# An MoE kernel on one core: the experts' results added in memory by the scatter, one scatter in flight

## The chip, the cores and the metric

The kernel runs on one core of a Trainium2 chip. The metric is device time in microseconds from the first to the last instruction of the launch, the median over runs. Times in the profile are those of one profiled execution.

## The reference, cut to what matters

One layer of a streaming encoder for 512 tokens of 1024 channels, in float32. First comes token mixing (projection, convolution branch, RWKV branch, merge), which the change leaves alone. Then a mixture of experts: every token picks 8 of 64 experts, each a SwiGLU of width 256, and a shared expert runs over all tokens.

```python
scores = jax.nn.sigmoid(t @ w_router)                  # choice: grouped top-8, gate = sel / sum * 2.5
expert(x) = (silu(x @ we_gate[e]) * (x @ we_up[e])) @ we_down[e]
routed = segment_sum(expert rows * gate, tok, 512)      # 512 x 8 = 4096 assignments
shared = (silu(t @ ws_gate) * (t @ ws_up)) @ ws_down
x = x + gt2 * rmsnorm(routed + shared, norm_ffn_post)
```

## The kernel before

The MoE part has four pieces, each a block of its own with a barrier at its end: `plan_experts` (buffers), `route`, `experts` and `combine`.

`route` computes scores, the choice of experts, the shared expert (kept in SBUF as `moe.shared`), and a table with three values for every token and expert: the gate, the token's number, and the number of the row 8 x token + rank in which this result is to be stored. Each value is split into three bfloat16 parts (`moe.parts`, L1795 to L1799), so that a product with a one-hot matrix picks it exactly. SP loads the weights of the first four experts at the end of this piece.

`experts` walks over blocks of up to 128 tokens of one expert: 64 first blocks, one for each expert, and a few more for experts with over 128 tokens (`n_blocks`, 68 with these inputs). A helper, `steps`, writes the same loop for every engine: a list of stages, each with a lead, so that in step b the stage of lead 4 works on block b+4. The order in the list is the order on the engine. For one block:

- DVE `places` and PE `numbers` (lead 4) pick the block's gates, token numbers and row numbers; DVE turns the last two into integers (`tokens`, `row_ids`). Places without a token get a number out of bounds, and the transfer skips them.
- POOL `gather` (lead 4, L2013): an indirect DMA reads the tokens' rows of 4 KB from memory into `xg`, one of four buffers.
- PE `turn_x`, ACT `x_high`, DVE `x_low` (lead 2): transpose, and split into a high and a low float32r part. ACT `high` and DVE `low` (lead 2) split the weights the same way; `low` writes over the loaded weights' place.
- PE `gate_up` (lead 1): 48 products of 512 columns a block; ACT and DVE make the hidden values; PE `down` (lead 0): 8 more. ACT and DVE copy the result to `y`, one of two buffers, and may do so when the scatter of two blocks before has landed (`left`).
- POOL `scatter` (lead 0, L2022): an indirect DMA writes the rows of `y` to their places in `moe.rows`, a tensor of 4096 rows in memory, so that no two writes meet. It waits for `y` and the row numbers, not for another scatter; two can be in flight. Ahead of every indirect DMA a tiny POOL operation on `carrier` carries its wait.

On POOL the order in a step is gather b+4, scatter b. In the blocks from 60 on, which may or may not exist, POOL also waits at the end of each step for the scatter's landing (`last`).

SP loads weights in a ring of four: it waits until PE is done with the gate and up of block n-4 and issues 2 MB for block n (L1863), then until PE is done with the down of block n-4 and issues 1 MB for block n (L1866), then the same for n+1. PE's gate and up run a block ahead of its down, so a down load and the next block's gate and up loads come right after each other. After the last block SP loads x1, the residual, 2 MB, into the place of ring slot 0 (L1995), which the profile names `x_again`, and waits for it.

`combine` (L2189): ten loads bring all 16 MB of `moe.rows` back, for each group of 128 tokens four rows a token for PE and four for DVE. PE adds its four and the shared expert by products with the identity, DVE adds its four in a tree, then the two. ACT squares, POOL takes the power for the norm, DVE scales by the gate row (`gated`) and adds to x1 (`finish`), and SP stores halves of 256 KB.

Of the kernel before, what the change touches and what calls it, by code (L numbers as in the profile page):

```python
# [28 lines left out]
P = 128  # L29
# [1506 lines left out]
NO_TOKEN, NO_ROW = 8 * S, 16 * S * TOPK  # L1536
# [3 lines left out]
def route(nc, w, keep, moe):  # L1540
# [4 lines left out]
    with ExitStack() as stack:  # L1545
# [29 lines left out]
        toki, tokf, pi, pf = m.sb("toki", [P, NT], I32), m.sb("tokf", [P, 3, NT]), m.sb("pi", [P, 1], I32), m.sb("pf", [P, 1])  # L1575
        iota_i = m.sb("iota_i", [P, S], I32)
        values = m.sb("table_values", [P, NT * NE, 3])
# [18 lines left out]
        def _(sp):  # L1596
# [7 lines left out]
            for b in range(moe.RING):  # L1604
                moe.load_gate_up(sp, b, b)
                moe.load_down(sp, b, b)

        @block.gpsimd
        def _(pool):
            pool.iota(toki[:, :], [[P, NT]], base=0, channel_multiplier=1).then_inc(s_io, 1)  # L1610
            pool.iota(pi[:, :], [[0, 1]], base=0, channel_multiplier=1).then_inc(s_io, 1)
            pool.iota(iota_i[:, :], [[1, S]], base=0, channel_multiplier=0).then_inc(s_io, 1)
            pool.memset(resets[:, :, :], 1.0).then_inc(s_io, 1)
            pool.memset(moe.offsets[:, 0:1], float(NO_TOKEN)).then_inc(s_io, 1)
            pool.memset(moe.offsets[:, 1:2], float(NO_ROW)).then_inc(s_io, 1)
            pool.wait_ge(s_io, 6)
            pool.memset(resets[:, :, 0:1], 0.0).then_inc(s_io, 1)

        @block.scalar
        def _(act):  # L1620
# [15 lines left out]
            for t in range(NT):  # L1636
# [8 lines left out]
                for half in range(2):  # L1645
                    act.activation(moe.shared[:, t, half * N:half * N + N], bank[6 + half][:, :], ACT.Copy).then_inc(s_dnA, 1)
# [74 lines left out]
        def _(dve):  # L1721
# [11 lines left out]
            dve.wait_ge(s_io, 7)  # L1733
# [6 lines left out]
            link.sign(V.tensor_scalar(tokf[:, 2, :], tokf[:, 0, :], float(TOPK), float(-NO_ROW), ALU.mult, ALU.add))  # L1740
# [43 lines left out]
            for t in range(NT):  # L1784
# [49 lines left out]
def plan_experts(nc, m, w, keep, moe):  # L1834

    moe.RING = 4
    with ExitStack() as first_use:
        raw = Memory(nc, first_use)
        gate_up = [moe.x1] + [raw.sb(f"gate_up{i}", [P, NT, D]) for i in range(1, moe.RING)]
    low = [moe.low0] + [m.sb(f"gate_up_low{i}", [P, 2, KD, DE], F32R) for i in range(1, moe.RING)]  # L1840
    moe.gate_up = [t[:, :, :].rearrange("p a d -> p (a d)").rearrange("p (j k n) -> p j k n", j=2, k=KD) for t in gate_up]
    moe.low = low
    moe.down = m.sb("down_ring", [P, moe.RING, 2, D])
    moe.place = m.sb("place", [P, NT, NE])
    moe.parts = m.sb("table_parts", [P, NT, NE, 3, 3], BF16)
# [4 lines left out]
    moe.offsets = m.sb("offsets", [P, 2])  # L1850
# [20 lines left out]
def experts(nc, w, keep, moe):  # L1871
# [4 lines left out]
    with ExitStack() as stack:  # L1876
# [3 lines left out]
        column = m.sb("column", [P, 2, NT, 9], BF16)  # L1880
        number = m.sb("number", [P, 4, 3])
        tokens = m.sb("tokens", [P, 4, 1], U32)
        row_ids = m.sb("row_ids", [P, 4, 1], U32)
# [17 lines left out]
        s_num, s_rows = m.sem("p5_token_numbers"), m.sem("p5_row_numbers")  # L1901
# [7 lines left out]
        s_x1 = m.sem("p5_x1_in")  # L1909
# [67 lines left out]
        def _(sp):  # L1977
            with sp.Fori(1, NE // RING) as turn:
                for u in range(RING):
# [3 lines left out]
                    moe.load_down(sp, RING * turn + u, u)  # L1983
            count = sp.value_load(moe.n_blocks[0:1, 0:1], min_val=NE, max_val=MAXB)
# [9 lines left out]
            sp.wait_ge(s_y, count)  # L1994
            sp.dma_start(moe.x1[:, :, :], keep.x1_dram.rearrange("(t p) d -> p t d", p=P)).then_inc(s_x1, 16)  # L1995
            sp.wait_ge(s_x1, 16)

        @block.gpsimd
        def _(pool):
            last_token, last_row = pool.to_reg(S - 1), pool.to_reg(S * TOPK - 1)  # L2000
# [63 lines left out]
        def _(pe):  # L2064
# [59 lines left out]
        def _(dve):  # L2124
# [31 lines left out]
            def numbers(b, u, first):  # L2156
# [3 lines left out]
                V.tensor_reduce(number[:, u % 4, :], pid[:, 0:9].rearrange("p (v j) -> p v j", j=3), AX.X, ALU.add).then_inc(s_sum, 1)  # L2160
# [3 lines left out]
            def row_numbers(b, u, first):  # L2164
                dve.wait_ge(s_num, b + 1)
                V.tensor_tensor(row_ids[:, u % 4, :], number[:, u % 4, 2:3], moe.offsets[:, 1:2], ALU.add).then_inc(s_rows, 1)
# [13 lines left out]
            def y_half(b, u, first):  # L2180
# [5 lines left out]
                        (1, row_numbers), (0, y_half)])  # L2186


def combine(nc, w, keep, moe, out):  # L2189

    with ExitStack() as stack:  # L2191
        m = Memory(nc, stack)
        H = TOPK // 2
        rows = m.sb("rows6", [P, NT, TOPK, D])
# [5 lines left out]
        bank = [m.bank(f"e{i}") for i in range(2 * NT)]  # L2200

        s_pe_in = [m.sem(f"p6_tensor_rows{t}_in") for t in range(NT + 1)]
        s_dve_in = [m.sem(f"p6_vector_rows{t}_in") for t in range(NT + 1)]
        s_sum = m.sem("p6_tensor_sum")
        s_pair, s_tree = m.sem("p6_pairs"), m.sem("p6_tree")
        s_y, s_gt = m.sem("p6_y"), m.sem("p6_y_gated")
# [4 lines left out]
        expert_rows = moe.rows.rearrange("(t p j) d -> t p j d", p=P, j=TOPK)  # L2211
        LAST = NT - 1
# [5 lines left out]
        def _(sp):  # L2218
            for t in range(LAST):
                sp.dma_start(rows[:, t, 0:H, :], expert_rows[t][:, 0:H, :]).then_inc(s_pe_in[t], 16)  # L2220
                sp.dma_start(rows[:, t, H:TOPK, :], expert_rows[t][:, H:TOPK, :]).then_inc(s_dve_in[t], 16)  # L2221
            for half in range(2):
                sp.dma_start(rows[:, LAST, 0:H, cols(half)], expert_rows[LAST][:, 0:H, cols(half)]).then_inc(s_pe_in[LAST + half], 16)
                sp.dma_start(rows[:, LAST, H:TOPK, cols(half)],
                             expert_rows[LAST][:, H:TOPK, cols(half)]).then_inc(s_dve_in[LAST + half], 16)
# [5 lines left out]

        @block.tensor
        def _(pe):
            for t in range(NT):
                for half in range(2):
                    pe.matmul(bank[2 * t + half][:, :], keep.ident[:, :], moe.shared[:, t, cols(half)], start=True, stop=False)
                    pe.wait_ge(s_pe_in[t + half if t == LAST else t], 16)
                    for j in range(H):
                        mm = pe.matmul(bank[2 * t + half][:, :], keep.ident[:, :], rows[:, t, j, cols(half)],
                                       start=False, stop=(j == H - 1))  # L2240
                    mm.then_inc(s_sum, 1)
# [8 lines left out]
        def _(act):  # L2250
            link = Link(act, s_a)
            for t in range(NT):
                act.wait_ge(s_y, 2 * t + 1)
# [5 lines left out]
                act.wait_ge(s_y, 2 * t + 2)  # L2259
# [4 lines left out]
        def _(dve):  # L2264
            V = nc.vector
            gt = keep.gate2
            trees = [0, 0]

            def tree(t, cs):

                V.tensor_tensor(rows[:, t, H:H + 2, cs], rows[:, t, H:H + 2, cs], rows[:, t, H + 2:TOPK, cs],  # L2271
                                ALU.add).then_inc(s_pair, 1)
                trees[0] += 1
                dve.wait_ge(s_pair, trees[0])
                V.tensor_tensor(rows[:, t, H, cs], rows[:, t, H, cs], rows[:, t, H + 1, cs], ALU.add).then_inc(s_tree, 1)  # L2275
                trees[1] += 1

            def add(t, half):

                dve.wait_ge(s_tree, trees[1])  # L2280
                dve.wait_ge(s_sum, 2 * t + half + 1)
                V.tensor_tensor(y[:, t, cols(half)], rows[:, t, H, cols(half)], bank[2 * t + half][:, :], ALU.add).then_inc(s_y, 1)  # L2282

            def gated(t, half):

                dve.wait_ge(s_y, 2 * t + half + 1)
# [10 lines left out]

            for t in range(LAST):
                dve.wait_ge(s_dve_in[t], 16)
                tree(t, slice(0, D))  # L2300
                for half in range(2):
                    add(t, half)
# [76 lines left out]
```

## Time and profile before

| | us |
|---|---|
| median of 3 runs | 1509.97 (1507.34 to 1515.13) |
| profiled execution | 1509.81 |
| its span, first to last instruction | 1508.0 |
| PE busy | 1352.0 (90%) |
| DVE busy | 1045.0 (69%) |
| ACT busy | 613.3 (41%) |
| POOL busy | 344.7 (23%) |
| mean granted clock of TensorE | 0.938 of 2.4 GHz |
| read from HBM, written | 334.40 MB, 44.04 MB |

The page of the profile gives busy time by engine, then the span in 40 slices of 37.7 us in tenths. Token mixing takes the first 17 slices, routing about two, the experts slices 20 to 38, `combine` the last one and a half. A busy PE is not PE at its peak: ends of matmuls are modelled. "DMA share" is the mean busy share of the 16 DMA engines. Moves by SP's queue are called hardware_dynamic, POOL's software_dynamic.

### The profile page before, as it was taken

The numbers are of one execution on the slowest core, as the hardware profiler recorded it, in microseconds if no ns is written. First come the engines' busy times: TensorE is split into PE (matmuls) and PEld (weight loads), VectorE is DVE, ScalarE is ACT, GpSimd is POOL, SyncE is SP. The second block draws the span as 40 slices with busy tenths as digits, with TensorE's granted clock in tenths as the row PEclk, the third lists the DMA queues.
The fourth block names the chain that finished last, engine by engine and source line by source line (L and its number), as shares of the span: only waits on it lengthen the run. The fifth ranks groups of instructions, "written<-read, shape, count | busy, mean of one in ns | idle before, by whom it ended". The sixth has DMA issues, their size and how long they took to land. (4 is left out here: it accounts for less than half of the span.)

```text
span 1508.0 us, 18807 instructions
## 1 busy us (share of the span) xinstructions
PE 1352.0 (90%) x5795; PEld 926.9 (61%) x5795; DVE 1045.0 (69%) x1646; ACT 613.3 (41%) x928; POOL 344.7 (23%) x350
## 2 busy tenths in 40 slices
PE   6799999965589799869699999999999999999947
PEld 3577676723589544344476777777777777776713
DVE  4539999959833252325688887887888888888617
ACT  3322222142123211211465565665665665655502
POOL 0344324133000000000223232232232333232200
PEclk9799999876699899979799999999999999999969
DMA  8343534110000440094289999989999988999358
GB/s 305 144 148 131 202 133 146 49 70 0 1 1 1 168 167 14 28 355 196 78 330 346 364 352 347 359 349 347 365 384 368 356 343 348 361 351 338 143 212 352
DMA packets 85841, 341.34 MB, mean 226 GB/s; under 512 B 16983, under 2 KB 20241, under 8 KB 58661
## 3 DMA queue, kind: packets, MB, share of 16 engines
q1 hardware_dynamic: 65976, 307.07, 53.2%
q0 software_dynamic: 19584, 33.60, 6.2%
q8 instruction: 27, 0.44, 0.1%
q14 instruction: 18, 0.14, 0.0%
q10 hardware_dynamic: 236, 0.09, 0.0%
HBM read 334.40 MB, written 44.04 MB: 251 GB/s over the span
## 5 line engine op out<-in xcount | busy, mean ns | idle before, releaser
L2144 DVE TENSOR_TENSOR gate_up_low<-gate_up,gate_up_high 128x1024 fp32r<-128x1024 f32 x204 | 245.3, 1223 | 47.2 <-ACT gate_up_high L2035 41.9
L2116 PE MATMUL py<-down_ring,hT 128*128 128x512 f32 x544 | 250.0, 602 | 0.9 <-ACT hT L2054 0.9
L2077 PE MATMUL p_gate_up<-gate_up_high,x_hi 128*128 128x512 f32 x544 | 242.7, 446 | 5.3 <-DVE x_lo L2153 5.3
L2077 PE MATMUL p_gate_up<-gate_up_low,x_hi 128*128 128x512 f32 x544 | 216.6, 398 | 0.0
L2077 PE MATMUL p_gate_up<-gate_up_high,x_lo 128*128 128x512 f32 x544 | 216.6, 398 | 0.0
L2035 ACT ACTIVATE gate_up_high<-gate_up 128x1024 fp32r<-128x1024 f32 x204 | 204.1, 1052 | 1.0 <-issue 0.8
L2116 PEld LDWEIGHTS py<-down_ring,hT 128*128 128x128 f32 x544 | 97.9, 190 | 98.8 <-issue 98.7
L2006 POOL TENSOR_TENSOR carrier<-offsets 1x1 f32<-1x1 f32 x136 | 28.7, 211 | 535.9 <-DVE tokens L2162 487.3
L269 POOL TENSOR_TENSOR ring_lo<-ring,w_hi 128x2048 fp32r<-128x2048 f32 x19 | 91.6, 4823 | 179.0 <-ACT w_hi L310 179.0
L2077 PEld LDWEIGHTS p_gate_up<-gate_up_high,x_hi 128*128 128x128 f32 x544 | 104.0, 191 | 45.6 <-issue 21.2
L429 PE MATMUL pz<-h_hi,w_hi 128*128 128x512 f32 x304 | 123.4, 406 | 7.7 <-DVE h_lo L497 7.7
L429 PE MATMUL pz<-h_lo,w_hi 128*128 128x512 f32 x304 | 122.1, 402 | 0.0
L2077 PEld LDWEIGHTS p_gate_up<-gate_up_high,x_lo 128*128 128x128 f32 x544 | 103.8, 191 | 29.8 <-issue 11.0
L429 PE MATMUL pz<-h_hi,ring_lo 128*128 128x512 f32 x304 | 122.1, 401 | 0.0
L2077 PEld LDWEIGHTS p_gate_up<-gate_up_low,x_hi 128*128 128x128 f32 x544 | 103.0, 189 | 24.1
L2022 POOL DMA_INDIRECT expert_rows<-y,row_ids x68 | 112.1, 1649 | 19.9 <-issue 19.9
L2059 ACT ACTIVATE y<-py 128x512 f32<-128x512 f32 x68 | 40.7, 599 | 179.4 <-PE py L2116 179.4
L510 DVE SCALAR_TENSOR_TENSOR co<-upad,taps,co 128x512 f32<-128x512 f32 x120 | 104.4, 936 | 0.0
L2144 DVE TENSOR_TENSOR gate_up_low<-x_again,gate_up_high 128x1024 fp32r<-128x1024 f32 x68 | 81.6, 1221 | 13.7 <-ACT gate_up_high L2035 12.9
L2048 ACT ACTIVATE x_hi<-px 128x512 fp32r<-128x512 f32 x136 | 73.9, 595 | 39.5 <-PE px L2090 39.5
L2153 DVE TENSOR_TENSOR x_lo<-px,x_hi 128x512 fp32r<-128x512 f32 x136 | 87.2, 683 | 1.6 <-ACT x_hi L2048 1.6
L459 DVE SCALAR_TENSOR_TENSOR ada_acc<-ring,silu_c,ada_acc 128x512 f32<-128x512 f32 x76 | 78.3, 1030 | 2.7
(363 smaller groups left out, 2034.8 us busy)
## 6 DMA issues: line engine op xcount, KB each, us to landing
down_ring<-in_we_down SPq DMA_DIRECT2D x68, 1024.0 KB, 8.7
gate_up<-in_we_gate SPq DMA_DIRECT2D x51, 1024.0 KB
gate_up<-in_we_up SPq DMA_DIRECT2D x51, 1024.0 KB
ring<-in_w_ada SPq DMA_DIRECT2D x12, 2048.0 KB, 8.1
ring<-in_w_in SPq DMA_DIRECT2D x9, 2048.0 KB, 10.4
x_again<-in_we_gate SPq DMA_DIRECT2D x17, 1024.0 KB
x_again<-in_we_up SPq DMA_DIRECT2D x17, 1024.0 KB
rows<-expert_rows SPq DMA_DIRECT2D x6, 2048.0 KB, 18.4
```

The costliest lines, as they stand in the source:

```text
L269: pool.tensor_tensor(pair(ring_lo, b), pair(ring, b), exact(w_hi[:, b % 2, :, :]), ALU.subtract).then_inc(s_wlo, 1)
L429: last = pe.matmul(pz[n % 3][:, :], weights, h[:, k, :], start=(k == 0 and i == 0), stop=(k == KD - 1 and i == 2))
L459: last = nc.vector.scalar_tensor_tensor(out=acc[:, i % 2, :], in0=ring[:, slot, k, :], scalar=c_k, in1=acc[:, i % 2, :], op0=ALU.mult, op1 ...
L510: done[r] = link.sign(nc.vector.scalar_tensor_tensor(out=mix.co[:, r, :], in0=u, scalar=tap, in1=mix.co[:, r, :], op0=ALU.mult, op1=ALU.add))
L2022: pool.indirect_dma_start(moe.rows, bass.IndirectOffsetOnAxis(row_ids[:, u % 4, 0:1], 0), y[:, u % 2, :], None, bounds_check=last_row, oob ...
L2035: act.activation(w_hi[:, u % 2, :, piece(i), :], moe.gate_up[u % RING][:, :, piece(i), :], ACT.Copy).then_inc(s_hi, 1)
L2048: act.activation(x_hi[:, u % 2, 4 * half:4 * half + 4, :], px[half][:, :].rearrange("p (k s) -> p k s", k=4), ACT.Copy).then_inc(s_xhi, 1)
L2059: act.activation(y[:, u % 2, 0:N], py[0][:, :], ACT.Copy).then_inc(s_yA, 1)
L2077: mm = pe.matmul(pgu[u % 2][:, :], x[:, u % 2, k, :], weights, start=(k == 0 and n == 0), stop=(k == KD - 1 and n == 2))
L2116: mm = pe.matmul(py[half][:, :], hT[:, u % 2, k, :], weights[:, k, half * N:half * N + N], start=(k == 0), stop=(k == 1))
L2144: V.tensor_tensor(moe.low[u % RING][:, :, piece(i), :], moe.gate_up[u % RING][:, :, piece(i), :], exact(w_hi[:, u % 2, :, piece(i), :]), A ...
L2153: V.tensor_tensor(x_lo[:, u % 2, ks, :], px[half][:, :].rearrange("p (k s) -> p k s", k=4), exact(x_hi[:, u % 2, ks, :]), ALU.subtract).th ...
```

## The change

There is no `moe.rows` any more. A tensor `moe.sums` of 512 rows in memory is set to the shared expert's result by four stores at the end of `route`, and each block's scatter adds its rows to it in memory. A block has a token once at most, but two blocks can hold the same token, so a scatter waits until the one before it has landed. The third table value goes. x1 is loaded in `experts`, after the loads of block 63 and ahead of those of the blocks from 64 on, into a buffer that is not part of the ring (in `route` it holds the shared result). `combine` loads 2 MB of sums and takes the norm. Cut to its core:

```diff
@@ route
-        scores, biased, sel, gated, left, rank, resets = (old(NT, NE) for _ in range(7))
+        scores, biased, sel, gated, left = (old(NT, NE) for _ in range(5))
+        shared = moe.x1
-        values = m.sb("table_values", [P, NT * NE, 3])
+        values = m.sb("table_values", [P, NT * NE, 2])
             for b in range(moe.RING):
                 moe.load_gate_up(sp, b, b)
                 moe.load_down(sp, b, b)
+            for t in range(NT):
+                sp.wait_ge(s_dnA, 2 * t + 2)
+                sp.dma_start(moe.sums[t * P:(t + 1) * P, :], shared[:, t, :]).then_inc(moe.s_base, 16)
-            link.sign(V.tensor_scalar(tokf[:, 2, :], tokf[:, 0, :], float(TOPK), float(-NO_ROW), ALU.mult, ALU.add))
-            link(V.tensor_tensor_scan(rank[:, :, :].rearrange("p t e -> p (t e)"), resets[:, :, :].rearrange("p t e -> p (t e)"),
-                                      sel[:, :, :].rearrange("p t e -> p (t e)"), 0.0, ALU.mult, ALU.add))
-            link(V.tensor_tensor(rank[:, :, :], rank[:, :, :], sel[:, :, :], ALU.subtract))
-            for t in range(NT):
-                link.sign(V.tensor_scalar(values[:, t * NE:(t + 1) * NE, 2], rank[:, t, :], tokf[:, 2, t:t + 1], None, ALU.add))
@@ plan_experts
-        gate_up = [moe.x1] + [raw.sb(f"gate_up{i}", [P, NT, D]) for i in range(1, moe.RING)]
+        gate_up = [raw.sb(f"gate_up{i}", [P, 2, KD, DE]) for i in range(moe.RING)]
-    moe.rows = nc.dram_tensor("expert_rows", (S * TOPK, D), F32, kind="Internal").ap()
+    moe.sums = nc.dram_tensor("expert_sums", (S, D), F32, kind="Internal").ap()
@@ experts, SP: after the loop over the first 64 blocks
+            sp.wait_ge(moe.s_base, 16 * NT)
+            sp.dma_start(moe.x1[:, :, :], keep.x1_dram.rearrange("(t p) d -> p t d", p=P)).then_inc(moe.s_x1, 16)
@@ experts, SP: at the end
-            sp.wait_ge(s_y, count)
-            sp.dma_start(moe.x1[:, :, :], keep.x1_dram.rearrange("(t p) d -> p t d", p=P)).then_inc(s_x1, 16)
-            sp.wait_ge(s_x1, 16)
@@ experts, POOL
             def scatter(b, u, first):
-                pool.wait_ge(s_rows, b + 1)
+                pool.wait_ge(s_target, b + 1)
                 pool.wait_ge(s_yA, b + 1)
                 pool.wait_ge(s_yV, b + 1)
+                if isinstance(b, int) and b == 0:
+                    pool.wait_ge(moe.s_base, 16 * NT)
+                if not (isinstance(b, int) and b == 0):
+                    scattered(pool, b - 1, (u - 1) % 4)
                 carry_wait(s_scatter, b, 1)
-                pool.indirect_dma_start(moe.rows, bass.IndirectOffsetOnAxis(row_ids[:, u % 4, 0:1], 0), y[:, u % 2, :], None,
-                                        bounds_check=last_row, oob_is_err=False).then_inc(s_out[u % 2], 16)
+                pool.indirect_dma_start(moe.sums, bass.IndirectOffsetOnAxis(targets[:, u % 4, 0:1], 0), y[:, u % 2, :], None,
+                                        bounds_check=last_token, oob_is_err=False, compute_op=ALU.add).then_inc(s_out[u % 2], 16)
@@ experts, PE and DVE: numbers
-                    mm = pe.matmul(pid[:, 0:9], hot[:, u % 2, t, :], column[:, u % 2, t, :], start=(t == 0), stop=(t == NT - 1))
+                    mm = pe.matmul(pid[:, 0:6], hot[:, u % 2, t, :], column[:, u % 2, t, :], start=(t == 0), stop=(t == NT - 1))
@@ combine (PE's part, the trees and the sums on DVE are gone)
-            for t in range(LAST):
-                sp.dma_start(rows[:, t, 0:H, :], expert_rows[t][:, 0:H, :]).then_inc(s_pe_in[t], 16)
-                sp.dma_start(rows[:, t, H:TOPK, :], expert_rows[t][:, H:TOPK, :]).then_inc(s_dve_in[t], 16)
+            for t in range(NT):
+                sp.dma_start(y[:, t, :], moe.sums[t * P:(t + 1) * P, :]).then_inc(s_in[t], 16)
+            for t in range(NT):
+                dve.wait_ge(s_in[t], 16)
                 for half in range(2):
                     gated(t, half)
-                finish(t)
+                if t:
+                    finish(t - 1)
+            finish(NT - 1)
```

## Rows read from the trace of the kernel before

**Rows 1.** The page: busy tenths of PE and DMA in 40 slices.

```profile
PE   6799999965589799869699999999999999999947
...
DMA  8343534110000440094289999989999988999358
```

**Rows 2.** Windows by stage: length, busy us (instructions) of each engine, clock, DMA.

```profile
755.94:1441.81 685.87, 682.68 (x3020) 483.19 (x3018) 548.99 (x907) 407.67 (x589) 200.99 (x260) 1.00 0.88 338
...
1441.80:1455.60 13.80, 0.00 (x0) 0.00 (x0) 0.00 (x0) 0.00 (x0) 0.99 (x1) 0.52 0.39 150
1455.60:1508.00 52.40, 38.28 (x80) 15.64 (x80) 30.02 (x34) 7.55 (x24) 2.20 (x4) 0.86 0.90 361
```

**Rows 3.** Timeline of the last stage: start, us, engine, line, operation [idle before].

```profile
1455.61 0.34 SPq L2220 DMA_DIRECT2D rows<-expert_rows  x1
...
1467.80 2.29 DVE L2271 TENSOR_TENSOR rows<-rows 128x2048 f32<-128x2048 f32 x1 [26.87 <-DMA rows<-expert_rows]
...
1472.10 0.63 ACT L2256 ACTIVATE sq<-y 128x512 f32<-128x512 f32 x1 [31.29 <-DVE y L2282]
...
1473.31 1.29 DVE L2287 SCALAR_TENSOR_TENSOR scaled<-y,gate_row 128x512 f32<-128x512 f32 x2
...
1475.18 1.41 DVE L2295 SCALAR_TENSOR_TENSOR x_again<-scaled,rstd,x_again 128x512 f32<-128x512 f32 x2 [0.58 <-POOL rstd L2247]
...
1504.09 1.41 DVE L2295 SCALAR_TENSOR_TENSOR x_again<-scaled,rstd,x_again 128x512 f32<-128x512 f32 x2 [0.53 <-POOL rstd L2247]
```

**Rows 4.** Timeline of SP's queue in the expert stage.

```profile
1002.16 0.33 SPq L1866 DMA_DIRECT2D down_ring<-in_we_down  x1
...
1012.49 0.33 SPq L1866 DMA_DIRECT2D down_ring<-in_we_down  x1
```

**Rows 5.** Timeline of POOL in the same block.

```profile
1002.55 1.02 POOL L2013 DMA_INDIRECT xg<-h_rows,tokens  x1 [0.45 <-issue]
...
1003.94 2.00 POOL L2022 DMA_INDIRECT expert_rows<-y,row_ids  x1 [0.16 <-issue]
```

**Rows 6.** Windows inside blocks; the last two numbers are DMA share and GB/s.

```profile
1004.00:1011.00 7.00, 7.00 (x35) 5.10 (x35) 6.53 (x9) 4.50 (x7) 1.95 (x1) 1.00 1.00 406
1011.50:1013.50 2.00, 2.00 (x9) 1.30 (x8) 1.22 (x5) 0.92 (x2) 0.82 (x2) 1.00 0.50 193
...
1114.80:1116.80 2.00, 2.00 (x9) 1.30 (x8) 1.16 (x5) 0.99 (x2) 1.24 (x3) 1.00 0.91 377
```

**Rows 7.** DMA queues: 1014.5 to 1016 (first two), then 1011.5 to 1013.5.

```profile
DMA packets 76, 0.62 MB, mean 415 GB/s; under 512 B 0, under 2 KB 0, under 8 KB 0
...
q1 hardware_dynamic: 76, 0.62, 101.4%
...
q0 software_dynamic: 67, 0.05, 7.5%
...
down_ring<-in_we_down SPq DMA_DIRECT2D x1, 1024.0 KB, 8.3
```

**Rows 8.** DMA issues: count, KB each, median us to landing.

```profile
xg<-h_rows SPq DMA_DIRECT2D x4, 512.0 KB, 5.1
```

**Rows 9.** Timeline at the end of routing.

```profile
708.03 0.42 DVE L1728 TENSOR_TENSOR sig<-sig,d 128x256 f32<-128x256 f32 x1 [5.65 <-ACT sig L1633]
...
717.15 1.09 ACT L1646 ACTIVATE shared<-d 128x512 f32<-128x512 f32 x2 [3.79 <-PE d L1689]
```

**Rows 10.** DMA queue of SP from 1440.4 to 1441.4, the x1 reload's start.

```profile
q1 hardware_dynamic: 8, 0.03, 36.8%
```

**Rows 11.** Timeline: the last gate load's issue, and ACT's first reading of it.

```profile
1396.58 0.33 SPq L1863 DMA_DIRECT2D gate_up<-in_we_gate  x1
...
1416.45 2.00 ACT L2035 ACTIVATE gate_up_high<-gate_up 128x1024 fp32r<-128x1024 f32 x2
```

**Rows 12.** Timeline of POOL in the tail, where it waits for its scatter.

```profile
1376.95 1.81 POOL L2022 DMA_INDIRECT expert_rows<-y,row_ids  x1 [0.16 <-issue]
...
1389.36 0.18 POOL L2006 TENSOR_TENSOR carrier<-offsets 1x1 f32<-1x1 f32 x1 [10.60 <-DMA expert_rows<-y,row_ids]
```

More of the change, by code:

```diff
@@ L1535 @@
 MAXB = NE + S * TOPK // P - 1
-NO_TOKEN, NO_ROW = 8 * S, 16 * S * TOPK
+NO_TOKEN = 8 * S
 BIG = 1e30
@@ L1612, in _ @@
             pool.iota(iota_i[:, :], [[1, S]], base=0, channel_multiplier=0).then_inc(s_io, 1)
[L1613 to L1617, printed above, removed]
+            pool.memset(moe.offsets[:, :], float(NO_TOKEN)).then_inc(s_io, 1)
         @block.scalar
@@ L1645, in _ @@
                 for half in range(2):
-                    act.activation(moe.shared[:, t, half * N:half * N + N], bank[6 + half][:, :], ACT.Copy).then_inc(s_dnA, 1)
+                    act.activation(shared[:, t, half * N:half * N + N], bank[6 + half][:, :], ACT.Copy).then_inc(s_dnA, 1)
         @block.tensor
@@ L1731, in hidden @@
                 V.tensor_tensor(gu[:, t % 2, :], sig[:, t % 2, :], bank[4 + t % 2][:, DE:2 * DE], ALU.mult).then_inc(s_sV, 1)
-            dve.wait_ge(s_io, 7)
+            dve.wait_ge(s_io, 4)
             link.sign(V.tensor_copy(tokf[:, 0, :], toki[:, :]))
@@ L1838, in plan_experts @@
         raw = Memory(nc, first_use)
-        gate_up = [moe.x1] + [raw.sb(f"gate_up{i}", [P, NT, D]) for i in range(1, moe.RING)]
-    low = [moe.low0] + [m.sb(f"gate_up_low{i}", [P, 2, KD, DE], F32R) for i in range(1, moe.RING)]
-    moe.gate_up = [t[:, :, :].rearrange("p a d -> p (a d)").rearrange("p (j k n) -> p j k n", j=2, k=KD) for t in gate_up]
-    moe.low = low
+        gate_up = [raw.sb(f"gate_up{i}", [P, 2, KD, DE]) for i in range(moe.RING)]
+    low = [m.sb(f"gate_up_low{i}", [P, 2, KD, DE], F32R) for i in range(moe.RING)]
+    moe.gate_up, moe.low = gate_up, low
     moe.down = m.sb("down_ring", [P, moe.RING, 2, D])
     moe.place = m.sb("place", [P, NT, NE])
-    moe.parts = m.sb("table_parts", [P, NT, NE, 3, 3], BF16)
+    moe.parts = m.sb("table_parts", [P, NT, NE, 2, 3], BF16)
     moe.iota = m.sb("iota", [P, S])
@@ L1849, in plan_experts @@
     moe.n_blocks = m.sb("n_blocks", [1, 1], I32)
[L1850 removed]
+    moe.offsets = m.sb("no_token", [P, 1])
     moe.s_gate_up = [m.sem(f"expert_gate_up{i}_in") for i in range(moe.RING)]
     moe.s_down = [m.sem(f"expert_down{i}_in") for i in range(moe.RING)]
[L1853 removed]
+    moe.sums = nc.dram_tensor("expert_sums", (S, D), F32, kind="Internal").ap()
     halves = [w["we_gate"][0].rearrange("e (p k) n -> e p k n", k=KD), w["we_up"][0].rearrange("e (p k) n -> e p k n", k=KD)]
@@ L1879, in experts @@
         hot = m.sb("hot", [P, 2, NT, P], BF16)
-        column = m.sb("column", [P, 2, NT, 9], BF16)
-        number = m.sb("number", [P, 4, 3])
+        column = m.sb("column", [P, 2, NT, 6], BF16)
+        number = m.sb("number", [P, 4, 2])
         tokens = m.sb("tokens", [P, 4, 1], U32)
-        row_ids = m.sb("row_ids", [P, 4, 1], U32)
+        targets = m.sb("targets", [P, 4, 1], U32)
         x_hi, x_lo = m.sb("x_hi", [P, 2, KD, P], F32R), m.sb("x_lo", [P, 2, KD, P], F32R)
@@ L1900, in experts @@
         s_sum = m.sem("p5_numbers_whole")
-        s_num, s_rows = m.sem("p5_token_numbers"), m.sem("p5_row_numbers")
+        s_num, s_target = m.sem("p5_token_numbers"), m.sem("p5_target_numbers")
         s_xg = [m.sem(f"p5_gathered{i}") for i in range(4)]
@@ L1993, in _ @@
                             moe.load_down(sp, expert, u)
-            sp.wait_ge(s_y, count)
-            sp.dma_start(moe.x1[:, :, :], keep.x1_dram.rearrange("(t p) d -> p t d", p=P)).then_inc(s_x1, 16)
-            sp.wait_ge(s_x1, 16)
         @block.gpsimd
         def _(pool):
-            last_token, last_row = pool.to_reg(S - 1), pool.to_reg(S * TOPK - 1)
+            last_token = pool.to_reg(S - 1)
             def carry_wait(semaphore, b, place):
@@ L2159, in numbers, with target_numbers @@
                 taken(dve, s_x, b, 4)
-                V.tensor_reduce(number[:, u % 4, :], pid[:, 0:9].rearrange("p (v j) -> p v j", j=3), AX.X, ALU.add).then_inc(s_sum, 1)
+                V.tensor_reduce(number[:, u % 4, :], pid[:, 0:6].rearrange("p (v j) -> p v j", j=3), AX.X, ALU.add).then_inc(s_sum, 1)
                 dve.wait_ge(s_sum, b + 1)
                 V.tensor_tensor(tokens[:, u % 4, :], number[:, u % 4, 1:2], moe.offsets[:, 0:1], ALU.add).then_inc(s_num, 1)
-            def row_numbers(b, u, first):
+            def target_numbers(b, u, first):
                 dve.wait_ge(s_num, b + 1)
-                V.tensor_tensor(row_ids[:, u % 4, :], number[:, u % 4, 2:3], moe.offsets[:, 1:2], ALU.add).then_inc(s_rows, 1)
+                V.tensor_tensor(targets[:, u % 4, :], number[:, u % 4, 1:2], moe.offsets[:, 0:1], ALU.add).then_inc(s_target, 1)
             def places(b, u, first):
@@ L2185, in _ @@
             steps(dve, [(2, low(0)), (2, low(1)), (4, places), (2, low(2)), (1, silu), (1, hidden), (2, low(3)), (2, x_low), (4, numbers),
-                        (1, row_numbers), (0, y_half)])
+                        (1, target_numbers), (0, y_half)])
 def combine(nc, w, keep, moe, out):
@@ L2192, in combine @@
         m = Memory(nc, stack)
-        H = TOPK // 2
-        rows = m.sb("rows6", [P, NT, TOPK, D])
         x1 = moe.x1
@@ L2199, in combine @@
         whole, rstd = m.sb("whole6", [P, NT]), m.sb("rstd6", [P, NT])
[L2200 to L2206, printed above, removed]
+        s_in = [m.sem(f"p6_sums{t}_in") for t in range(NT)]
+        s_gt = m.sem("p6_y_gated")
         s_half, s_whole, s_r = m.sem("p6_half_squares"), m.sem("p6_squares"), m.sem("p6_rstd")
@@ L2210, in combine @@
         block = stack.enter_context(nc.Block())
-        expert_rows = moe.rows.rearrange("(t p j) d -> t p j d", p=P, j=TOPK)
-        LAST = NT - 1
         def cols(half):
@@ L2218, in _ @@
         def _(sp):
-            for t in range(LAST):
-                sp.dma_start(rows[:, t, 0:H, :], expert_rows[t][:, 0:H, :]).then_inc(s_pe_in[t], 16)
-                sp.dma_start(rows[:, t, H:TOPK, :], expert_rows[t][:, H:TOPK, :]).then_inc(s_dve_in[t], 16)
[L2222 to L2225, printed above, removed]
+            for t in range(NT):
+                sp.dma_start(y[:, t, :], moe.sums[t * P:(t + 1) * P, :]).then_inc(s_in[t], 16)
             for t in range(NT):
@@ L2230, in _ @@
             sp.wait_ge(s_st, 16 * 2 * NT)
[L2232 to L2241, printed above, removed]
         @block.gpsimd
@@ L2252, in _ @@
             for t in range(NT):
-                act.wait_ge(s_y, 2 * t + 1)
+                act.wait_ge(s_in[t], 16)
                 if t:
@@ L2266, in _ @@
             gt = keep.gate2
[L2267 to L2282, printed above, removed]
+            dve.wait_ge(moe.s_x1, 16)
             def gated(t, half):
-                dve.wait_ge(s_y, 2 * t + half + 1)
                 V.scalar_tensor_tensor(out=scaled[:, t, cols(half)], in0=y[:, t, cols(half)], scalar=D ** 0.5, in1=gt[:, cols(half)],
@@ L2296, in finish @@
                                            in1=x1[:, t, cols(half)], op0=ALU.mult, op1=ALU.add).then_inc(s_o, 1)
[L2298 to L2302, printed above, removed]
+            for t in range(NT):
+                dve.wait_ge(s_in[t], 16)
                 for half in range(2):
                     gated(t, half)
-                finish(t)
-            for half in range(2):
-                dve.wait_ge(s_dve_in[LAST + half], 16)
-                tree(LAST, cols(half))
-                add(LAST, half)
-            for half in range(2):
-                gated(LAST, half)
-            finish(LAST)
+                if t:
+                    finish(t - 1)
+            finish(NT - 1)
 class Names:
@@ L2345, in layer @@
         moe = Names()
-        moe.shared = m.sb("shared", [P, NT, D])
-        with ExitStack() as first_use:
-            moe.x1 = Memory(nc, first_use).sb("x1_again", [P, NT, D])
-        moe.low0 = m.sb("gate_up_low0", [P, 2, KD, DE], F32R)
+        moe.x1 = m.sb("x1_again", [P, NT, D])
+        moe.s_base, moe.s_x1 = m.sem("sums_set"), m.sem("x1_again_in")
         with ExitStack() as moe_stack:
```

4 lines of the change are left out of this document (1 added, 3 removed).

## The prediction, made before the changed kernel ran

> **What bounds the kernel now.** I read the page's 40 slices first, then the windows by stage, then the traffic inside one expert block. In the slices the second half of the span is one stage with PE at 9 tenths and the DMA engines at 8 or 9 at the same time [rows 1]. The windows give the edges: from the first scatter at 755.94 to the last at 1441.81 PE is busy 682.68 of 685.87 us at granted clock 1.00, with the DMA engines at 0.88 and 338 GB/s; after it come 13.80 us without a matmul, and 52.40 us of the last stage, with DMA at 0.90 and 361 GB/s [rows 2]. So the expert stage is PE's and the last stage is a transfer: DVE idles 26.87 us before its first row sum, for rows to land [rows 3].
>
> PE being full doesn't say that DMA has room, so I looked inside a block. The down load is issued at 1002.16 and again at 1012.49: a block is 10.33 us [rows 4]. In SP's order the gate and up loads follow the down load at once, so all 3 MB of a block's weights are issued together, and POOL's gather and scatter within 2 us of them [rows 5]. From 1004 to 1011 all 16 DMA engines work (share 1.00); from 1011.5 to 1013.5 the share is 0.50, and 67 packets of POOL's queue are still draining [rows 6, 7]. I read this as two halves: a block has 4096/68 = 60 real rows of 128, they lie in the first partitions, so all real gather and scatter rows fall to eight engines. Each of those eight carries in a block 3 MB/16 = 24 packets of 8 KB, eight gathered rows and eight scattered rows of 4 KB. A weight packet takes 0.320 us (76 packets at 101.4% of 16 engines in 1.5 us [rows 7]), a 4 KB row half, 0.160. That is 24 x 0.320 + 16 x 0.160 = 10.24 us in a block of 10.33; the other eight have 7.7. The mean of 0.88 hides that half the DMA engines are as full as PE. In some blocks no quiet window is seen at all (share 0.91 at 1114.8 [rows 6]).
>
> **The change, part by part.**
>
> *The last stage gets short.* Gone are 16 MB of row reads, the sums on PE and the trees on DVE; in place come four loads of 512 KB. They can't start earlier than the first does now, at 1455.61 [rows 3], when the last scatter has landed and the block has closed. A 512 KB load of the same form took 5.1 us at the median of four in one queue [rows 8]; for the first of four I take 3.3, tile 0 at 1458.9. ACT's squares and POOL's power take 3.08 us (1472.10 to 1475.18 [rows 3]), so DVE can finish tile 0 from 1462.0, with two tiles gated before it. From there four finishes of 1.41 and two gatings of 1.29 [rows 3] are 8.2: DVE is done at 1470.2. The last store takes what it takes now, 1508.0 - 1505.5 = 2.5 [rows 3]. End at 1472.7, **-35 us**; an adding scatter may land 1 us later, so -34. The x1 reload ends before the block closes today; taking it from there saves nothing.
>
> *Routing.* The rank scan, its subtraction, five scalar operations and a third of the table splits go from DVE, about 3.5 us of work (an estimate from their sizes). PE covers it: DVE waits 5.65 us after the table for the fourth tile's sigmoid [rows 9]. Without that cover it would be a gain of 3. Four 512 KB stores are added on SP; the last waits for ACT's last copy, which ends at 718.24 [rows 9], so the block may close 0.5 us later. They land behind the first weights, with until 755.9 to do it. 0 for both.
>
> *In a block.* The number product has 6 columns for 9, DVE reduces 2 values for 3, the target number replaces the row number: under 0.1 us on engines other than PE's weight stream, 0.
>
> *The scatter now adds.* The trace has no adding transfer, so I bound a row's price. From below: 0.160 us as now, the destination's read riding beside the source's. In the middle: a second 4 KB through the same engine, 0.320. From above: 4 KB packets that don't stream, the first eight of the x1 reload on idle engines, 16 x 0.368 / 8 = 0.74 us each [rows 10]. I take 0.320: within a stream a packet here costs by its bytes, and the destination is 4 KB more on the same engine. The loaded engines have eight such rows: 10.24 + 8 x 0.160 = 11.52 us. Against that, in the open blocks engines stand idle for 0.1 to 0.3 us before the next burst, so 10.24 may be 10.0 and the sum 11.3. I use 11.38, **1.05 us over PE's 10.33**. The Trainium skill ("Collectives: The Full Stack", Part 3, the bandwidth ceiling) says that the add in a DMA engine is not what slows a reducing transfer: it needs two source reads for one write, and runs at half the rate. By that rule a row is 0.320 as well, and it speaks against the change, since it puts the price on the engines without room. No run here shows it yet.
>
> From scatter 0 to the last weights there are some 63 such blocks: 66 us. Part is absorbed. The last block's gate load is issued at 1396.58 and ACT first reads it at 1416.45 [rows 11]: 20 us, of which landing now uses about 11 (a down load takes 8.3, and POOL's queue is empty by 1014.5, 11 us after the burst [rows 7]). 9 us of lateness are free, then ACT waits for gate_up and PE behind it. 66 - 9 = **+57**. The x1 reload, now inside the stage, is 2 MB/16 = 32 rows of 4 KB an engine, **+5** as no engine has room for it; with room it would be 0.
>
> *One scatter in flight.* POOL now waits for scatter b-1 before it issues b, and behind it on POOL stands gather b+5. In the tail, where POOL waits for its scatter already, issue to landing was 12.41 us (1376.95 to 1389.36 [rows 12]); the scatter of 1003.94 drains until about 1014 [rows 5, 7], 10 us or a little more. So a landing is as long as a block, and POOL will wait in nearly all of them. But its queue is first in, first out: scatter b stands behind gather b+4, issued 1.4 us before it [rows 5], and that gather's eight rows with weight packets between them drain only from 4 us on. Issued 1 to 3 us later, the scatter lands when it would have. The y buffers allow two blocks, the gather has over one to its transpose. I count 0; the rival below is the case in which the cover goes.
>
> Sum, against the profiled run (1509.81, its span 1508.0; the median of the three is 1509.97, no different): 1509.8 - 34 + 57 + 5 = **1538**.
>
> **The rivals.**
> 1. *The add rides free.* A row stays near 0.160, the block at 10.33, x1 fits in: 1509.8 - 34 = 1476. For it: PE is full today, and the DMA share is 0.88 [rows 2]. Against: the destination's read must cost an engine nothing. It turns to the other side from 0.6 us a block on (34 less 5 for x1, plus 9 of cover, over 63), a row price of 0.24.
> 2. *The wait is the bound.* If the next scatter is issued only when the queue is empty and nothing fills its start, a block lasts one landing, 12.4 us by the longest row [rows 12]: 2.1 x 63 = 130, less a block of cover, 1509.8 - 34 + 120 = 1596. For it: a landing is at the block's length already and an adding one is longer. Against: the gather's rows fill the new scatter's start.
> 3. *The destination's read doesn't stream.* 0.74 us a row, 8 x 0.58 = 4.6 us a block, less 9: 1509.8 - 34 + 290 - 9 = 1757. For it, only that HBM answers late on idle engines [rows 10]; against it, that every other transfer streams.
>
> Stalls of 1 us a block on PE could also cost clock. It was 1.00 over a stage with 3 us of idle in all [rows 2], so the trace can't price it; it is in the range.
>
> **How the numbers follow.** Forecast 0.42, its own range 1505 to 1570 (packet price and slack); rival 1 0.25; rival 2 0.20; rival 3 and worse 0.13. The range takes in the first two rivals and leaves out the third: 1474 to 1640. One measurement of this kernel tells about 0.5%, 7.5 us, from no change. Faster: rival 1 and 0.04 of the forecast's low end, 0.29; same 0.07; slower 0.64.
>
> **What would show it.** Right: in the expert stage the interval of the down loads is about 11.4 us, the quiet window's share goes from 0.5 to near 1, PE is at 0.91 and ACT or PE wait for the gate_up load, POOL waits 1 to 4 us a block for its scatter, and from the first load of sums to the end there are 17 us, not 52. Wrong: a block of 10.33 with POOL's waits there (rival 1); a block as long as POOL's issue-to-landing with DMA engines idle between (rival 2); several times today's DMA time per row of POOL's queue (rival 3).

## The result, and the profile after

| | us |
|---|---|
| before, median of 5 runs | 1509.97 (1507.34 to 1515.13) |
| after, median of 5 runs | 1525.07 (1523.39 to 1531.87) |
| ratio | 1.0103, 95% interval 1.0072 to 1.0134 |
| profiled execution after, its span | 1531.87, 1529.8 |

The change makes the kernel 1% slower. 1538 was forecast, with 1505 to 1570 as the forecast's own range. Of the 21.8 us between the two profiled spans, 4.5 are there before the expert stage begins (first scatter at 760.42, not 755.94). I don't put that part down to the change: over the kernels below, none of which touches what comes before routing, it begins anywhere from 750.9 to 763.6.

The page after, the slices and the two DMA queues; they answer to [rows 1]. The last line is POOL's queue on the page of the kernel before:

```profile
PE   6899999955599799778799999999999999999890
...
DMA  8343634110000530294399998988999988889833
...
q1 hardware_dynamic: 64152, 294.48, 49.9%
q0 software_dynamic: 19584, 33.62, 8.8%
```

```profile
q0 software_dynamic: 19584, 33.60, 6.2%
```

The slices look alike; the second queue doesn't. POOL's queue moves the same 19584 packets and the same megabytes as before, and took 6.2% of 16 engines' span then, 8.8% now. That is (0.088 x 1529.8 - 0.062 x 1508.0) x 16 = 658 us over 4096 added rows: **0.161 us more for a row**, the price taken in the prediction's sum. The rounding of the shares makes that 0.155 to 0.167, and the same working between the kernels below gives up to 0.20 (the spread rows against the plain write, 9.5% of 1471.0 against 6.1% of 1472.3). The trace also keeps the duration of every packet. In the kernel before, the 8192 packets of 4 KB in POOL's queue take 0.159 us at the median. After, the shorter half still takes 0.159, the gather's rows, and the longer half 0.327, the scatter's. The medians are the same in every kernel below that adds, so a row costs 0.168 us more.

The same three stages as in [rows 2], with the same columns:

```profile
760.42:1500.53 740.11, 698.14 (x3019) 480.93 (x3017) 539.92 (x907) 400.17 (x589) 206.52 (x261) 1.00 0.87 316
1500.53:1513.10 12.57, 0.00 (x0) 0.00 (x0) 0.00 (x0) 0.00 (x0) 1.56 (x1) 0.53 0.02 2
1513.10:1529.80 16.70, 0.00 (x0) 0.00 (x0) 10.38 (x16) 7.11 (x24) 3.08 (x4) 0.50 0.67 251
```

The expert stage went from 685.87 to 740.11 us, +54.2, and PE now idles 42 us in it, at a granted clock of still 1.00. From the last scatter to the end it was 66.2 and is 29.3, -36.9. The 12.57 us between the stages have a DMA share of 0.02, where the x1 reload used to run: as forecast, taking it from there saved next to nothing.

What the engines wait for from 755 us on: who, for whom, us in total, times, longest.

```profile
POOL carrier L1997 <- DMA expert_sums<-y,targets: 479.0, 65, 10.5
DVE gate_up_low L2139 <- ACT gate_up_high L2030: 150.4, 65, 7.8
...
ACT gate_up_high L2030 <- DMA gate_up<-in_we_up: 103.2, 51, 7.4
...
ACT y L2054 <- DMA expert_sums<-y,targets: 62.2, 17, 4.8
```

Three waits are new, and the profile alone doesn't say which of them sets the block. POOL waits 479 us for its scatter, more than any engine for anything; ACT waits 103 us for weights, and DVE behind it; and ACT waits 62 us, in 17 blocks, until the scatter of two blocks before has left its buffer of `y`. They fit the forecast and its second rival alike.

The last stage, first the sums' loads, then ACT, then DVE's first and last finish; it answers to [rows 3]:

```profile
1513.12 1.75 SPq L2207 DMA_DIRECT2D y<-expert_sums  x4
1516.38 0.63 ACT L2227 ACTIVATE sq<-y 128x512 f32<-128x512 f32 x1 [19.43 <-DMA y<-expert_sums]
...
1519.51 1.41 DVE L2249 SCALAR_TENSOR_TENSOR x_again<-scaled,rstd,x_again 128x512 f32<-128x512 f32 x2 [0.47 <-POOL rstd L2218]
...
1524.58 2.73 DVE L2249 SCALAR_TENSOR_TENSOR x_again<-scaled,rstd,x_again 128x512 f32<-128x512 f32 x4
```

Tile 0 lands 3.3 us after the first load, DVE is done 14.2 us after it, and the stage takes 16.7 us, where 17.1 was worked out.

DMA issues after, median us to landing in the last column, and last the down load in the kernel before:

```profile
down_ring<-in_we_down SPq DMA_DIRECT2D x68, 1024.0 KB, 17.4
...
x_again<-x_rows SPq DMA_DIRECT2D x1, 2048.0 KB, 23.7
```

```profile
down_ring<-in_we_down SPq DMA_DIRECT2D x68, 1024.0 KB, 8.7
```

### The profile page after: what moved, and what is told of

The parts are those of the page before. It is cut to its first block and busy times, and to the rows that moved or that the text cites. A ratio compares the mean times of both kernels' runs of the same rounds, so it can differ in the third digit from the quotient of the medians.

```text
span 1529.8 us, 18673 instructions
## 1 busy us (share of the span) xinstructions
PE 1332.1 (87%) x5715; PEld 911.4 (60%) x5715; DVE 1013.1 (66%) x1621; ACT 605.3 (40%) x928; POOL 352.7 (23%) x347
## 3 DMA queue, kind: packets, MB, share of 16 engines
q0 software_dynamic: 19584, 33.62, 8.8%
## 5 line engine op out<-in xcount | busy, mean ns | idle before, releaser
L2139 DVE TENSOR_TENSOR gate_up_low<-gate_up,gate_up_high 128x1024 fp32r<-128x1024 f32 x272 | 326.0, 1219 | 155.2 <-ACT gate_up_high L2030 153.4
L2030 ACT ACTIVATE gate_up_high<-gate_up 128x1024 fp32r<-128x1024 f32 x272 | 272.0, 1050 | 105.8 <-DMA gate_up<-in_we_up 103.2
L2072 PE MATMUL p_gate_up<-gate_up_high,x_hi 128*128 128x512 f32 x544 | 229.1, 421 | 32.2 <-DVE x_lo L2148 32.0
L1997 POOL TENSOR_TENSOR carrier<-no_token 1x1 f32<-1x1 f32 x136 | 53.9, 396 | 596.7 <-DMA expert_sums<-y,targets 479.0
L2017 POOL DMA_INDIRECT expert_sums<-y,targets x68 | 112.0, 1647 | 12.6 <-issue 12.1
L2004 POOL DMA_INDIRECT xg<-h_rows,tokens x68 | 74.7, 1099 | 19.8 <-issue 11.7
```

The lines of the kernel that those rows point to most:

```text
L2004: pool.indirect_dma_start(moe.xg[:, u % 4, :], None, keep.h2_dram, bass.IndirectOffsetOnAxis(tokens[:, u % 4, 0:1], 0), bounds_check=last_ ...
L2017: pool.indirect_dma_start(moe.sums, bass.IndirectOffsetOnAxis(targets[:, u % 4, 0:1], 0), y[:, u % 2, :], None, bounds_check=last_token, o ...
L2030: act.activation(w_hi[:, u % 2, :, piece(i), :], moe.gate_up[u % RING][:, :, piece(i), :], ACT.Copy).then_inc(s_hi, 1)
L2072: mm = pe.matmul(pgu[u % 2][:, :], x[:, u % 2, k, :], weights, start=(k == 0 and n == 0), stop=(k == KD - 1 and n == 2))
L2139: V.tensor_tensor(moe.low[u % RING][:, :, piece(i), :], moe.gate_up[u % RING][:, :, piece(i), :], exact(w_hi[:, u % 2, :, piece(i), :]), A ...
```

## The experiments

Theory A is the forecast: eight of the 16 DMA engines have all real rows of POOL's queue, and are over a block's time once a row costs double. Theory B: the landing of a scatter, waited for each block, is the block. A block's length is read from ACT's copies of `y`, the first at the start of the stage and the one of block 59, 59 blocks later: 754.38 and 1363.57 before, 758.80 and 1409.43 after, so 10.33 and 11.03 us. It comes from the one profiled execution of each kernel. The ratios are to the kernel before, run on the same chip.

| kernel | median us | ratio (95% interval) | block, us |
|---|---|---|---|
| after | 1525.07 | 1.0103 (1.0072 to 1.0134) | 11.03 |
| two sums, two scatters in flight | 1545.14 | 1.025 (1.020 to 1.030) | 11.24 |
| plain write, no addition | 1474.18 | 0.976 (0.970 to 0.982) | 10.30 |
| rows spread over partitions | 1469.99 | 0.974 (0.968 to 0.979) | 10.28 |
| before, with the wait alone | 1513.04 | 1.002 (0.999 to 1.005) | 10.33 |
| after, x1 loaded last | 1531.49 | 1.016 (1.012 to 1.019) | 11.02 |
| spread, x1 loaded last | 1468.29 | 0.975 (0.971 to 0.979) | 10.28 |
| before, rows spread | 1508.89 | 0.998 (0.995 to 1.001) | 10.33 |
| two sums and spread | 1479.63 | 0.980 (0.977 to 0.983) | 10.28 |
| second and third quarter exchanged | 1473.23 | 0.972 (0.969 to 0.976) | 10.27 |

### Is it the wait? Two sums in turn

```diff
-                    scattered(pool, b - 1, (u - 1) % 4)
+                    scattered(pool, b - 2, u % 2)
-                pool.indirect_dma_start(moe.sums, ...)
+                pool.indirect_dma_start(moe.sums[u % 2], ...)
```

> The changed kernel with two sums in memory, even blocks into one and odd blocks into the other, each set to half of the shared result; a scatter waits for the one two blocks before, so two are in flight. combine loads both (4 MB) and adds them on DVE. Theory A (eight DMA engines are full: weights plus eight gathered and eight adding rows each): the wait was not the bound, a block stays at 11.1 us, and the second 2 MB of sums cost 5 us: about 1530. Theory B (the wait for the landing sets the block): the block goes back to 10.33, 59 x 0.8 = 47 us off, 5 us on: about 1483.

It got slower, not faster, by more than A's 5 us. Windows of this kernel from its first to its 60th block, and what ACT waited for up to 1420 us:

```profile
750.80:1413.90 663.10, 625.63 (x2715) 430.84 (x2713) 486.86 (x823) 359.96 (x532) 181.95 (x235) 1.00 0.90 326
```

```profile
ACT gate_up_high L2031 <- DMA gate_up<-in_we_up: 120.6, 52, 3.3
```

POOL's wait for a scatter is gone from the list of waits in the loop, and so is ACT's for a free `y`. ACT's wait for weights isn't: 120.6 us, 52 times. B falls. Of the 20 us over the changed kernel, the end has 7 (36.4 us from the last scatter on, not 29.3) and the 59 blocks 12, both by the profiled executions: with two adding scatters in flight a block is 0.2 us longer. Why is open; it wasn't tried apart.

### Is it the wait? The kernel before with the wait alone

```diff
+                if not (isinstance(b, int) and b == 0):
+                    scattered(pool, b - 1, (u - 1) % 4)
                 carry_wait(s_scatter, b, 1)
```

> The kernel before with one thing from the change: a scatter waits until the one before it has landed. Plain writes to 4096 rows, the old last stage. The prediction's zero for the wait: landings of 11 us include the time behind the gather, the scatter issued later lands when it would have, so 1510, ratio 1.000. Theory B: a landing of 10 to 11.4 us is longer than the block, each block 0.2 to 1 us longer: 1520 to 1570.

Its waits up to 1420 us, and its copies of `y` at both ends of the 59 blocks:

```profile
POOL carrier L2006 <- DMA expert_rows<-y,row_ids: 176.5, 62, 8.6
```

```profile
762.00 0.60 ACT L2061 ACTIVATE y<-py 128x512 f32<-128x512 f32 x1 [2.53 <-PE py L2118]
...
1371.19 0.60 ACT L2061 ACTIVATE y<-py 128x512 f32<-128x512 f32 x1 [2.62 <-PE py L2118]
```

POOL now waits 2.8 us in each block, and the block stays at 10.33. The prediction's zero for the wait holds: the landing adapts. I explain it by the queue's order (issued later, it stands behind less of the gather's traffic); that part was argued, not measured apart.

### Is it the addition? A plain write

```diff
-                                        bounds_check=last_token, oob_is_err=False, compute_op=ALU.add).then_inc(s_out[u % 2], 16)
+                                        bounds_check=last_token, oob_is_err=False).then_inc(s_out[u % 2], 16)
```

> The changed kernel with the addition left out: the scatter overwrites rows of the 512-row tensor (the sum over experts isn't computed), still one in flight. Theory A: a row is 0.16 us again, the loaded engines have 10.2 us of work in a block, and the block is 10.33 to 10.4: about 1478. Theory B: a landing is 1.3 us shorter, which also lets the block fall to 10.33 to 10.5: 1478 to 1488. A third theory, that another part of the change (the x1 reload, the stores of the base) costs the time and not the addition, keeps it at 1520 or more.

This kernel leaves the sum over the experts out; all else of the change is in place and the block is 10.30 us. So the addition costs the time, 1525 - 1474 = 51 us of it, and the base's stores don't. The x1 reload does cost something here: ACT waits for the weights of block 64, issued behind it,

```profile
1389.21 2.01 ACT L2030 ACTIVATE gate_up_high<-gate_up 128x1024 fp32r<-128x1024 f32 x2 [3.77 <-DMA gate_up<-in_we_up]
```

and from block 59's `y` to the last one it takes 80.5 us, 3.9 more than before the change. What is left of the change is worth 2.4%.

### Is it the load of eight engines? Rows spread over the partitions

`hot` compares a token's place in the block with `moe.iota`; with the values permuted inside each 128, the same tokens lie on other partitions.

```diff
-            link.sign(V.tensor_copy(moe.iota[:, :], iota_i[:, :]))
+            link.sign(V.tensor_copy(moe.iota[:, :].rearrange("p (g h r) -> p g r h", g=NT, r=2),
+                                    iota_i[:, :].rearrange("p (g r h) -> p g r h", g=NT, r=2)))
```

> The changed kernel with the one-hot places permuted, so that a block's real rows lie on even partitions first, then on odd ones, and all 16 DMA engines carry four gathered and four adding rows each, not eight of them eight. Nothing else differs. Theory A: 24 x 0.32 + 4 x 0.16 + 4 x 0.33 = 9.6 us an engine, under 10.33: block 10.33, about 1478. Theory B with a landing set by fixed latency and turns in the queue, not by bytes: a landing is as long as now, block 11.1, 1525.

300 us of the expert stage in the kernel before, in the changed one and in this one (length, PE, PEld, DVE, ACT, POOL, clock, DMA share, GB/s):

```profile
900.00:1200.00 300.00, 300.00 (x1339) 213.41 (x1338) 244.28 (x406) 181.88 (x263) 91.83 (x118) 1.00 0.93 359
```

```profile
900.00:1200.00 300.00, 284.48 (x1238) 195.65 (x1237) 222.98 (x378) 164.76 (x243) 80.05 (x107) 1.00 0.92 334
```

```profile
900.00:1200.00 300.00, 300.00 (x1346) 214.32 (x1345) 244.83 (x408) 183.06 (x263) 106.78 (x117) 1.00 0.99 361
```

The reader should compare the last three numbers of each. The changed kernel moved 334 GB/s at a share of 0.92, and PE starved. With the same traffic spread, the share is 0.99, 361 GB/s are moved and PE is busy in all 300 us. A share of 0.92 was not 8% of room: it was some engines full and others not. This is also the fastest kernel so far: 1470, the addition and the single scatter in flight kept. POOL still waits for its scatter in 63 blocks up to 1420 us (221.7 us in all), and apart from one wait of 1.3 us of PE for a gather no other engine waits for a transfer of POOL's:

```profile
POOL carrier L1998 <- DMA expert_sums<-y,targets: 221.7, 63, 9.2
```

The kernel before with the same permutation tells that it is worth nothing by itself:

> The kernel before with only the places spread. Its loaded engines have 10.2 us of work in a block of 10.33, so PE is the bound and nothing is to be won: 1509, ratio 0.998 to 1.002. If DMA engines already cost time before (blocks held up by late weights), up to 1% faster: 1495.

0.998 (0.995 to 1.001). Before, the full engines were just not over.

### Which partitions share an engine? Two quarters exchanged

```diff
+            for g in range(NT):
+                link.sign(V.tensor_copy(moe.iota[:, g * P:(g + 1) * P].rearrange("p (a b h) -> p b a h", a=2, b=2),
+                                        iota_i[:, g * P:(g + 1) * P].rearrange("p (b a h) -> p b a h", a=2, b=2)))
```

> The changed kernel with the second and third quarter of a block's 128 places exchanged, so that 60 real rows lie in partitions 0 to 31 and 64 to 91. Asks which partitions share a DMA engine. If an engine has eight neighbouring partitions (0 to 7, 8 to 15, ...), eight engines still have eight rows each and nothing changes: block 11.1, 1525. If an engine has two groups of four, 32 partitions apart within a half (0 to 3 with 32 to 35), all 16 now have about four: block 10.3, 1470, as with the even spread.

1473, a block of 10.27 us:

```profile
900.00:1200.00 300.00, 300.00 (x1350) 214.20 (x1349) 245.35 (x410) 182.53 (x264) 97.75 (x118) 1.00 1.00 364
```

With real rows in partitions 0 to 31 and 64 to 91 the share is 1.00. So an engine doesn't have eight neighbours; the result fits two groups of four, 32 partitions apart, with the halves of 64 on different engines. The Trainium skill ("DMA: Bandwidth & Descriptors", the descriptor swizzle) gives this assignment for a transfer to 128 partitions; the trace agrees as far as this exchange and the even spread (0.99) can tell, and other groupings that share out both alike aren't excluded.

### What does the x1 reload cost?

The last load of [rows 11] has its counterpart in the changed kernel, where x1 is issued in front of the gate and up loads of block 64. ACT, reading them:

```profile
1441.00 2.00 ACT L2030 ACTIVATE gate_up_high<-gate_up 128x1024 fp32r<-128x1024 f32 x2 [7.40 <-DMA gate_up<-in_we_up]
```

I put the reload after all weights.

> The changed kernel, but x1 is loaded after the loads of the last blocks, as before (into its own buffer). In the changed kernel's trace ACT waits 7.4 us in one step for the gate_up load of block 64, issued behind the 2 MB of x1, and that step takes 18.8 us, not 11. If the full engines are the cause of that step, it goes: 5 to 8 us off, 1517 to 1520, and the blocks stay at 11.1. If the step comes from the tail's branches, no difference: 1525.

ACT's wait is gone, and nothing was gained: 1531 against 1525, with intervals that overlap. The timeline of PE in this kernel shows what stood behind it:

```profile
1443.15 1.16 PE L2085 MATMUL px<-ident,xg 128*128 128x128 f32 x8 [2.09 <-DMA xg<-h_rows,tokens]
1458.38 1.97 PE L2085 MATMUL px<-ident,xg 128*128 128x128 f32 x8 [4.69 <-DMA xg<-h_rows,tokens]
```

In the tail POOL waits for each scatter's landing before the next gather, as it did before the change, and here two gathers are late for PE, by 6.8 us in all; I put that down to longer landings while the engines are full, which wasn't tried apart. From block 59's `y` to the last one it takes 86.9 us in the changed kernel and 88.2 here; before it was 76.6. So the tail costs 10 us more, and moving x1 only changes which wait shows. With spread rows the same move was tried once more:

> Spread places and x1 last, together. With the spread alone no step was lost at the x1 reload, so there should be nothing more to win: 1470, within 2 us of the spread alone. If the reload still costs 5 us where the engines are even: 1465.

1468 and 1470 can't be told apart. The tail takes 77.6 us with x1 in front of block 64 and 76.2 with x1 last, so with even engines the reload costs 1 us or so.

### Both at once

> Two sums in turn and spread places. Engines at 9.6 us in a block; neither the load nor the wait is left, so a block is PE's 10.3. The last stage reads 4 MB, adds on DVE: 5 to 8 us more than with one sum, 1475 to 1480. If one scatter in flight still cost something with even engines, it would be under 1470.

1480, a block of 10.28: with even engines one scatter in flight costs nothing that a second one gives back, and the second sum costs its 2 MB and a DVE addition a tile.

## Why the prediction was right, and where its terms were off

- *The last stage, -34.* Right: 36.9. The stage is 16.7 us for 17.1, and the extra microsecond for an adding scatter's landing wasn't needed. The scatter's issue to the block's close even went from 13.80 to 12.57 us.
- *A row's price, 0.160 more.* Right: 0.161 from the page's queue shares, 0.168 from the packets' medians. Rival 3 is out, and rival 1 with it: the plain write shows what a free addition would give, 1474 measured, 1476 worked out for it.
- *Eight loaded engines.* Shown: two different permutations that spread the rows bring the block back to 10.28, with the addition in place.
- *1.05 us a block over PE.* Mis-sized. In the changed kernel the first blocks still take 10.3 us and the later ones 11.13 on average: 0.8 over PE. The prediction has 10.10 us of work before the change and 1.28 for the addition. The packets of the trace say which is off. A weight packet of 8 KB takes 0.309 us at the median, in quiet and in full stretches alike, not 0.320. (The mean is higher, 0.333, but packets of one engine overlap, as shares over 1.00 show, so means can't be added up.) And no block is like another: counted between two issues of a scatter, the first 60 blocks have 14 to 128 real rows, 62.7 on average, and 19 of them have more than 64. By the assignment of the quarters' section the fullest engine gets 7.6 rows of each kind a block, the eighth 5.3 (blocks 8 to 59). An estimate for the fullest from these medians is 24 x 0.309 + 7.6 x 0.318 = 9.8 us before, and 7.6 x 0.168 = 1.28 more, 11.1, after, which is the block measured. So the addition was sized right, and the slack before was 0.5 us where I had 0.2. "Eight engines with eight rows" is a simplification: the fullest ones set the time, since ACT waits for a whole load.
- *In a block, 0.* Not quite: with the load off the engines the new block is 10.27 to 10.30 us, not 10.33. Over 59 blocks that is 3 us in the change's favour.
- *9 us of cover.* About right: the first seven blocks stay at 10.3, which at 0.8 a block is 6 us. In the 59 blocks +41.4 us came out (650.6 for 609.2). The 57 forecast were for 63 blocks, 53 of them for these 59.
- *+5 for the x1 reload.* Open in the changed kernel: the reload delays weights as described, by 7.4 us, but loading x1 last gains nothing, since late gathers stand right behind it. In the plain write, whose full engines have some slack, it costs about 4 us, with even engines 1. The tail as a whole costs 10 us, and 2.6 us more pass between the last `y` and the last scatter: 13, where the prediction has 4 for four blocks and 5 for x1. Together the stage is +54, near the 62 expected. Part of that nearness is luck: the 59 blocks came out 12 lower, the tail 4 higher. How the tail's 10 us divide between late weights and late gathers wasn't measured apart.
- *The wait at 0.* Right, by the kernel before with the wait alone (1.002), and by two sums, which didn't help. Rival 2 falls, though POOL's wait is the longest of the new profile.
- *Clock.* PE's idle of 15.5 us in 300 cost none: granted clock 1.00 in the stage.

The signs that were named ahead came out less well than the sum. The down loads come 11.0 us apart where about 11.4 was said, PE is busy 0.94 of the stage (0.91 was said), and ACT waits for the gate and up loads. Two signs failed: POOL waits 7.4 us a block, not 1 to 4, and the quiet window's share didn't go to near 1. Two down loads, and a window ahead of the second, with the columns of [rows 6]:

```profile
1008.59 0.33 SPq L1859 DMA_DIRECT2D down_ring<-in_we_down  x1
...
1019.91 0.33 SPq L1859 DMA_DIRECT2D down_ring<-in_we_down  x1
```

```profile
1018.00:1020.00 2.00, 1.88 (x5) 0.57 (x3) 2.00 (x3) 0.00 (x0) 1.18 (x2) 1.00 0.50 205
```

A dearer row on the full engines couldn't fill this window: the engines with few real rows still finish early, so about half stay idle in it. And in size, the medians differ by 15 us and the profiled spans by 21.8, 4.5 of them before the stage, where 28 was forecast.

## What to carry to other kernels

A mean DMA share hides which engines it is made of. Where a transfer has real data on some partitions only, look at a window late in the period: a share that falls to a half while a queue still drains can mean that half of the engines have all of it. Those aren't the bound yet (before the change they weren't), but they are the first to become it; permuting the rows tells. Before a transfer is made dearer, spread its rows; here that was one permuted copy and turned +1% into -2.6%. And the longest wait in a profile isn't the cause for being the longest: POOL waited for its scatter in the kernels with even engines as well, with nobody behind it.

## What the hardware showed that I had not expected

- A mean DMA share of 0.99 to 1.00 over 300 us did not hold PE up at all: it was busy in all 300 of them. Such a share isn't a full one, since overlapping packets push it over 1.00: in the kernel with spread rows 2 us have 1.03 and, 4 us later, 0.76.
- Two adding scatters in flight, to different tensors, gave a block of 11.24 us, one in flight 11.03. The cause stays open.
- The addition cost a row of 4 KB no more than a second packet of that size would, 0.168 us more at the median where a plain row takes 0.159, with scattered rows of memory as the destination.
